# Softmax scaling, low weight parts and three other steps moved in a hybrid RWKV-7 and windowed-attention block

## What is computed

```python
h = rmsnorm(x, norm_gain)
proj = h @ w_in                      # 6528 columns: RWKV part, then attention part
y_rwkv = rwkv7_group(proj[:, :4224]) # 16 heads of 64, a state of 64 x 64 per head
y_attn = swa_sink_alibi_group(...)   # 16 query heads, 2 key heads, window 128, sinks
x = x + concat(y_rwkv, y_attn) @ w_out
return rmsnorm(x, final_gain)

# rwkv7, per head and token
sa = -S @ kk_t
S = S * w_t + outer(sa, b_t) + outer(v_t, k_t);   y = S @ r_t

# attention, per block of 128 queries over 256 keys
s = q @ k.T * 64 ** -0.5 - slope * dist           # masked outside the window
prob = softmax(concat(s, sink))[..., :-1];        o = prob @ v
```

## Time and profile before

| | before |
|---|---|
| median of 3 runs | 2111.14 us (2109.51 to 2116.64) |
| the profiled execution, its own time | 2108.85 us |
| its span, first to last instruction | 2107.1 us |
| PE busy | 1989.0 us (94%) |
| PE weight loads busy | 1559.5 us (74%) |
| DVE busy | 1296.9 us (62%) |
| ACT busy | 766.9 us (36%) |
| POOL busy | 279.0 us (13%) |
| mean granted clock of TensorE | 0.975 |
| the 6432 matmuls of L1095 on the chain that ended last | 58% of the span |

### The profile page before, as it was taken

One profiled execution on the slowest core, in us unless ns is written; L12 is line 12 of the kernel. 1 busy time (PEld: TensorE's weight loads), 2 busy tenths in 40 slices (PEclk: granted clock), 3 DMA queues, 4 the chain that ended last, 5 costly groups with the idle time before them and its releaser, 6 DMA issues.

```text
span 2107.1 us, 40075 instructions
## 1 busy us (share of the span) xinstructions
PE 1989.0 (94%) x15982; PEld 1559.5 (74%) x15982; DVE 1296.9 (62%) x2496; ACT 766.9 (36%) x1438; POOL 279.0 (13%) x592
## 2 busy tenths in 40 slices
PE   8999999999999999999999999999999989999995
PEld 5877777777777777777777777767777767887883
DVE  5656666666666666666666666666666665436434
ACT  6443423342434243433333424242424342324321
POOL 0010202020202020021111202020202021110112
PEclk9999999999999999999999999999999999999997
DMA  5532222222232224322322222222222333446542
GB/s 172 180 80 76 64 77 73 74 67 83 59 87 63 84 74 126 105 76 65 81 69 76 70 76 65 81 68 78 63 82 65 120 108 100 121 133 212 169 121 105
DMA packets 165643, 197.36 MB, mean 94 GB/s; under 512 B 70096, under 2 KB 73168, under 8 KB 165456
## 3 DMA queue, kind: packets, MB, share of 16 engines
q1 hardware_dynamic: 165456, 194.79, 32.0%
HBM read 174.79 MB, written 19.92 MB: 92 GB/s over the span
## 4 chain that ended last, share of the span: by engine, by line
PE 77%; DVE 11%; DMA 3%; ACT 3%; issue 2%; SPq 2%; POOL 2%; DVEq 0%; ACTq 0%; POOLq 0%
PE psum L1095 58%; PE psum L1080 3%; DVE w_lo L680 3%; PE psum L1248 2%; ACT w_hi L498 2%; PE psum L1203 2%; PE psum L1164 1%; PE psum L1229 1%; PE psum L1355 1%; PE psum L1239 1%; SPq L348 1%; POOL xt L447 1%; DVE score L877 1%; POOL x L445 1%; PE psum L1315 1%
## 5 line engine op out<-in xcount | busy, mean ns | idle before, releaser
L1095 PE MATMUL psum<-x_hi,w_hi 128*128 128x512 f32 x2144 | 896.8, 418 | 10.5 <-DVE x_lo L689 7.6
L1095 PE MATMUL psum<-x_hi,w_lo 128*128 128x512 f32 x2144 | 842.5, 393 | 0.0
L1095 PE MATMUL psum<-x_lo,w_hi 128*128 128x512 f32 x2144 | 841.8, 393 | 0.0
L680 DVE TENSOR_TENSOR w_lo<-w_raw,w_hi 128x512 fp32r<-128x512 f32 x536 | 373.7, 698 | 595.6 <-ACT w_hi L498 580.2
L498 ACT ACTIVATE w_hi<-w_raw 128x512 fp32r<-128x512 f32 x536 | 335.8, 630 | 1084.3 <-PE psum L1095 1058.8
L1095 PEld LDWEIGHTS psum<-x_hi,w_hi 128*128 128x128 f32 x2144 | 405.9, 189 | 133.5 <-issue 33.7
L1095 PEld LDWEIGHTS psum<-x_hi,w_lo 128*128 128x128 f32 x2144 | 405.4, 189 | 90.2
L1095 PEld LDWEIGHTS psum<-x_lo,w_hi 128*128 128x128 f32 x2144 | 406.8, 190 | 79.1 <-issue 7.7
L439 POOL COPY xt<-sub_ident 64x256 f32<-64x256 f32 x16 | 6.2, 390 | 1115.4 <-DMA x<-scratch_L 1115.4
L447 POOL TENSOR_TENSOR xt<-xt,x 64x15 f32<-64x15 f32 (+7 forms) x240 | 98.8, 412 | 18.8
L1080 PE MATMUL psum<-cst,score 128*128 128x128 f32 x256 | 44.3, 330 | 56.3 <-DVEq L879 56.3
(11 more groups left out here) (239 smaller groups left out, 1995.0 us busy)
## 6 DMA issues: line engine op xcount, KB each, us to landing
w_raw<-in_w_in SPq DMA_DIRECT2D x408, 256.0 KB, 2.7
w_raw<-in_w_out SPq DMA_DIRECT2D x128, 256.0 KB, 2.6
stage<-in_x_t SPq DMA_DIRECT2D x20, 256.0 KB, 3.3
stage<-scratch_MIX SPq DMA_DIRECT2D x19, 256.0 KB, 4.1
x_t<-scratch_X SPq DMA_DIRECT2D x256, 4.0 KB, 1.6
scratch_MIX<-sa SPq DMA_DIRECT2D x16, 256.0 KB, 3.1
scratch_MIX<-ym SPq DMA_DIRECT2D x16, 256.0 KB, 3.1
lora<-in_x_t SPq DMA_DIRECT2D x16, 256.0 KB, 2.9
```

What stands on the lines that cost most here:

```text
L680: nc.vector.tensor_tensor(w_lo[gq % SPLIT][:], w_raw[gq % RAW][:], w_hi[gq % SPLIT][:].bitcast(F32), ALU.subtract).then_inc(w_ready, 1)
L1095: mm = nc.tensor.matmul(psum[:, s % 2], wt[gq % SPLIT][:, cols], xx[:, c], start=(c == 0 and wt is w_hi and xx is x_hi), stop=(c == KC - 1 ...
```

## The change

- `low` goes from VectorE to GpSimd in the quarters in which the younger pair's `at` is 19 to 23 and there is a previous pair: 5 quarters of each of the 16 intervals, 80 of 536. GpSimd signals with a semaphore of its own; SyncE's loads and TensorE's quarters wait on the one that applies.
- The three operations of quarter 7 that scale `k` (L778 to L780) go to quarter 8, where they stand behind `softmax_norm`.
- The mix pair goes from `at` 32 to `at` 33 (quarter 9, ahead of the second round's scores), and the store of its result from `at` 34 to 35.
- The shift of v goes from quarter 10 to 11, behind `attended` and ahead of the norms' reciprocals; the eviction stays in 10.

```diff
+        w_ready_pool = sem("w_ready_pool")
+        def pool_low(gq):
+            return any(j >= 1 and 19 <= at < 24 for j, at in current(gq - 4))
+        def lows(gq, by_pool):
+            return sum(pool_low(x) == by_pool for x in range(gq + 1))
 # SyncE, load_w
-                        sp.wait_ge(w_ready, gq - RAW + 1)
+                        done = gq - RAW
+                        sp.wait_ge(w_ready_pool if pool_low(done) else w_ready, lows(done, pool_low(done)))
-                    if at == 34:
+                    if at == 35:
                         sp.wait_ge(mix_ready, i + 1)
 # GpSimd, at the head of each quarter
+                    x = gq + 4
+                    if x < QUARTERS and pool_low(x):
+                        pool.wait_ge(w_high, x + 1)
+                        nc.gpsimd.tensor_tensor(w_lo[x % SPLIT][:], w_raw[x % RAW][:], w_hi[x % SPLIT][:].bitcast(F32),
+                                                ALU.subtract).then_inc(w_ready_pool, 1)
 # VectorE, channels
+                    if at == 8:
                         then(nc.vector.tensor_scalar(a, a, 1.0, p(n, "k_a"), ALU.subtract, ALU.mult))
                         then(nc.vector.scalar_tensor_tensor(a, a, 1.0, k, ALU.add, ALU.mult))
                         then(nc.vector.tensor_tensor(kb[:, :, 0:4:3], a.rearrange(chunks, b=NB, c=2),
                                                      grow.rearrange(chunks, b=NB, c=2), ALU.mult))
                     if at == 10:
-                        shifted(tile_of(j, V_T), h, 4 * n + 1, v[:], p(n, "mu_v"))
+                        evicted(tile_of(j, V_T), h, 4 * n + 1)
+                    if at == 11:
+                        shift(v[:], p(n, "mu_v"))
 # VectorE, recurrence: the mix pair
-                    if at == 32:
+                    if at == 33:
                         dve.wait_ge(yt_full, i + 1)
 # VectorE, at the head of each quarter
-                    if gq + 4 < QUARTERS:
+                    if gq + 4 < QUARTERS and not pool_low(gq + 4):
                         low(gq + 4)
 # TensorE, quarter
-                    pe.wait_ge(w_ready, gq + 1)
+                    pe.wait_ge(w_ready_pool if pool_low(gq) else w_ready, lows(gq, pool_low(gq)))
```

## The result

The changed kernel took 2057.02 us (median of 4 runs, 2054.93 to 2064.54), beside 2110.32 us for the kernel before on the same chip: a ratio of 0.9748, with a 95% interval of 0.9730 to 0.9765. The profiled execution took 2057.9 us, 51.0 less than the profiled execution of before, at a granted clock of 0.988 instead of 0.975. The prediction was 2063.3 for that execution and 2065.5 on the scale of the median, in a range of 2035 to 2093.

The account below looks back on a forecast made before the run. TensorE, busy 94% of the span, bounds the kernel; only its waits and slow stretches can be won. 23.8 + 19.6 + 9.6 - 7.4 = 45.6 us off 2108.85 gives 2063.3 (2065.5 on the median's scale), range 2035 to 2093.

Parts of the forecast that it names:

- What is late next: Behind quarter 9's wait: GpSimd's inversion, its store and 24 small transfers; new waits in quarter 12, 1 to 3 us each.
- no wait of L1355: Sign for the chain of states: TensorE's weight loads no longer wait for VectorE's link; eight links in 11.2 us.
- Rival B: Small transfers don't bind, because GpSimd ends much earlier: gain 105 us, time 2006; chance 0.06.
- The links: Chain of states: with `low` on GpSimd odd links start earlier; 16 x 1.49 = 23.8 us gained.
- Rival C: Chain links aren't freed, as GpSimd's reading or start holds VectorE up: 23.8 us missing, time 2089; chance 0.07.
- `low` on GpSimd: Low parts on GpSimd lie on no path: cost nothing, at most 0.7 us four times an interval.
- The path from s: From last small transfer's issue (s) to quarter 15: turn at s+5.8, 24.0 us gained, 4.4 lost, net 19.6.
- What shifts s: GpSimd's last copy, less disturbed by VectorE, lets small transfers end 0.6 us earlier: 9.6 us (0 to 19).
- The moved steps: Operations on k, mix pair, its store and shift of v in later places on VectorE and the queue: no cost.
- The clock: TensorE pauses in quarter 12: 7 slow stretches of 3.4 us, 7.4 us lost (0 to 44); mean clock above 0.975.
- Rival A: Pauses of quarter 12 bring slow clock nearly everywhere, half 6.8 us long: 30 us lost, time 2088; chance 0.20.
- D: Slower: pauses in quarters 9, 12, 13, 15 keep TensorE at half clock 10.2 us an interval: time 2140; chance 0.05.

Follow-up runs that it names:

- The first experiment: Changed kernel with all moved steps put back, so only the low parts go to GpSimd: 2087.44 us, ratio 0.9896 to the kernel before.

## Why the prediction was right, point by point

**What is late next: right.** The sum of TensorE's waits fell by less than the two lines of the earlier trace rows: 56.3 + 39.0 = 95.3 before, 16.1 + 22.9 + 13.8 = 52.8 after. The 22.9 that came in is the transfers' path of the earlier trace rows. That the path limits, and was hidden before, is shown by what one edit brings in the two kernels, 31.7 and 6.3 us. (Of the 52.8 us, 13.8 are the two changes of phase, which the prediction left out when it named "no wait of L1355" as a sign.) Rival B (2006) would have needed the path away.

**The links: right in mechanism, the term 3.6 us too large.** 23.8 predicted, 20.2 measured. The step that was mis-sized is the factor 16. I wrote that I counted no gain at the change of halves beyond the 1.49; there was not even that, since another operation than `low` decides there, and there are two such intervals, not one. 14 x 1.49 is 20.9. Rival C (2089) fell. The first experiment isolates the term.

**`low` on GpSimd: right, no cost for the links.** No link was held beside GpSimd: the group of links has 283 ns in the mean over 112, and had 281; 60 of the 112 ran from start to end while GpSimd was at a subtraction, and none of these took more than 285 ns. By the rule of the Trainium skill (SBUF — State Buffer, Who interferes with whom) as the prediction read it, an operation with one input in PSUM is not blocked; the operation at 703.60 agrees, with 0.28 us. Operations of VectorE with both inputs in SBUF were held beside it, but only four overlapped with one of its subtractions, at the changes of phase (L704 and L707): they took 1.18 to 1.28 us instead of 0.69 to 0.75, 2 us in all.

**The path from s: right in mechanism, three terms off, all the same way.** Predicted 24.0 - 4.4 - 7.4 = 12.2 us, clock included; measured 21.4 - 3.0 = 18.4. Where nothing disturbs, the turn stands at s + 5.66 to 5.79, 5.70 in the mean, where I had taken 5.8 from the two intervals that showed it: 1.6 us more gained. The step that was mis-sized most is the clock: I expected 7 slow stretches from a mean wait of 1.9 us in quarter 12. The mean was 22.9 / 16 = 1.43 us, and four waits were over 2.0. Why the waits were half a microsecond shorter than I expected was not taken apart. In the four intervals with a slow stretch the turn came 1.0 us later than in the others, as in the price that I had set for one (1.05), so four cost 4.2 us instead of the 7.4 for seven. The level of quarter 15 cost 3.0 instead of 4.4 us: I had taken 12 more intervals with 8.68 us, and it was nine more and one less, since behind a slow stretch it stays at 8.30 to 8.33.

**What shifts s: right in size, the reason only in part.** 9.6 us estimated, 11.1 measured, and the edit on k is what brings it: with these operations back, all of it is gone (12.6 us). But I had named only GpSimd's last copy. That gave 2.6 us of it (16 copies, 14.5 us before and 11.9 after); the other 8.5 came from the small operations ahead of it (98.8 to 92.5 us and 90.7 to 88.5), for which the prediction had no term. That the size came out is partly luck.

**The moved steps: right, no cost** for the shift of v (2064.95 beside 2067.6). For the mix pair, only an exchange of waits is shown, and no cost of its place.

**The clock: right in direction.** 0.988 instead of 0.975. Rival A (2088) needed a slow stretch nearly everywhere, and D (2140) several in one interval. Neither came.

**The sum.** 45.6 predicted, 51.0 measured: -3.6 from the links, +6.2 from the path with its clock, +1.5 from the inversion, +1.3 from what I had at nothing. The last is within what two executions differ by.

## What to carry to other kernels

A waits view names only what comes last; look for intervals in which that wait happens to be short, since they show which path is late next and at what distance, and so how much of the wait can be won. When two paths run side by side at nearly the same length, an edit of one of them shows its worth only after the other is shortened (6.3 us, then 31.7), so test such edits again after each gain. And ask of an in-order engine what stands ahead of each short operation that another engine waits for: a subtraction that is slower elsewhere (1.29 against 0.69 us) was worth moving, and so was a mere change of order.

## What the runs showed of the hardware that I had not expected

The length of a wait did not settle whether a slow stretch follows. In the changed kernel waits from 2.02 us up were followed by one in quarter 12, and up to 1.76 us were not. But in the version with the links first a wait of 3.42 us was not followed and ones of 1.98 and 1.95 us were, and in the second profile of the changed kernel one of 2.23 us was not. I found no sharp line, and this remains open.

The stretches that came in the intervals were 3.4 or 6.8 us long, at half clock. Since some of them come or stay away by tenths of a microsecond in a wait, the changed kernel's time differs by 10 us from one measurement to another (2057.0 and 2067.6), more than the kernel before (2110.3 and 2111.0). That this is the cause is not shown, and the second profile speaks against it as the whole: only three waits of quarter 12 were followed by a slow stretch there. Of the 6.3 us between the two profiled executions 4.3 lie between the last link and the next inversion, spread over the intervals, 1.2 behind the last interval, and 0.8 on the whole way from the inversion to the last link. This remains open.

Two engines that issue at once hardly hold each other up: a small transfer took 11.92 / 24 = 0.50 us on SyncE alone, and 8.26 / 16 = 0.52 us with ScalarE beside it. ScalarE took 0.84 / 2 = 0.42 us for each of its first two and 3.74 / 6 = 0.62 us for the six others; why these are longer was not looked into.

A VectorE operation with one input in PSUM and one in SBUF ran undisturbed inside GpSimd's subtraction of two operands in SBUF: 284 ns in the mean of 60, while VectorE's operations with both inputs in SBUF took 1.18 to 1.36 us beside GpSimd instead of 0.69 to 0.75.
